# A two-block network on one core: the odd block's projection and its gated linear attention in one phase

## The chip, the cores and the metric

The kernel runs on one core of a Trainium2 chip. TensorE (PE) multiplies matrices, VectorE (DVE), ScalarE (ACT) and GpSimd (POOL) work on elements, SyncE (SP) issues transfers. Each engine takes its instructions in order and waits on semaphores. The metric is the device time of the whole program in microseconds. Before the change the median of three runs is 1949.43 us (1949.24 to 1950.46).

## The reference

Two networks in a row on 256 tokens of width 1024, all in f32: a block of attention and a block of state-space scan with their context, and then a second network of two layers. The change lies in the odd layer of the second one, of which the mixer is this (4 heads, keys of 128, values of 256, chunks of 64, gate rank 16):

```python
def gla_mixer(h, w_in, w_a2, b_a, head_g, w_out):
    z = h @ w_in
    q, k, v, r, ga = jnp.split(z, [hk, 2 * hk, 2 * hk + hv, 2 * hk + 2 * hv], axis=-1)
    log_a = jax.nn.log_sigmoid((ga @ w_a2 + b_a).astype(jnp.float32)) / C_TAU
    o = gla_chunked(heads(q, C_DK) * (C_DK ** -0.5), heads(k, C_DK), heads(v, C_DV), heads(log_a, C_DK))
    o = rms_norm(o, head_g)
    o = o.transpose(0, 2, 1, 3).reshape(Bn, S, hv) * jax.nn.silu(r.astype(jnp.float32))
    return o.astype(h.dtype) @ w_out

# gla_chunked, per chunk of 64 tokens; b = cumsum(log_a) in the chunk
    q_t, k_t, k_s = q * jnp.exp(b), k * jnp.exp(-b), k * jnp.exp(b_last - b)
    attn = jnp.where(causal, q_t @ k_t.T, 0.0)
    o = attn @ v + q_t @ state          # state of the chunks before
    state = exp(b_last) * state + k_s.T @ v
```

Here h is the RMS norm of x. The layer then adds the result to x and runs a convolutional feed-forward network (FFN) over it.

## The kernel before

The program is a chain of phases. Each phase has its own tiles and semaphores, and the next begins when all engines are through. Around the change they are: ffn0 (the FFN of the even layer), odin (the odd layer's input projection, `project`), gla (the attention, `gla`), odout (the output projection, `project_residual`) and ffn1 (`conv_ffn`).

**Products.** Large products run through `Split`. An f32 weight tile of 1024 x 512 lies in one of the two slots of a ring. For each half of it (four of the eight k tiles) ScalarE writes a rounded copy w_lead (L274, `lead`), and VectorE the remainder w_rest (L280, `rest`). x is parted the same way. TensorE then runs three matmuls for one exact product, lead by lead, lead by rest and rest by lead (L363). A group is one weight tile and gives 512 output columns; a half group is 24 matmuls (4 k tiles, 2 token tiles, 3 passes). odin has six groups: q, k, two of v, two of r. There is one buffer for each half of w_lead and w_rest, so the w_lead of a half can be written only when TensorE is through with the same half of the group before. SP loads the next tile into a ring slot as soon as both its w_rest are made. `empty` (L2161) takes a group out of PSUM into zz, with Identity for q, k, v and Silu for r.

**Start of a projection.** TensorE transposes x (L415), ScalarE makes x_lead (L424) and VectorE x_rest (L431). The first half of the first weights has been parted in the phase before: `EarlyHalf`, w_lead on ScalarE (L393) and w_rest on POOL (L397).

**The gates' inputs.** h @ w_ga has 16 columns. It stands behind the last group in odin as f32 matmuls (L2140), then ScalarE copies it to gaT.

**gla.** Its six small tables are loaded at the start of the phase. Then, each step waiting for the one before: gates (PE L2496), log-sigmoid (DVE L2551 to L2559, ACT Exp L2618 and Ln L2620), sums in the chunk (PE L2500, L2501), decays (PE L2504), exponentials (ACT L2623, L2624), q and k scaled (DVE L2563 to L2572), transposes (PE L2511, ACT L2635). Then four heads one after the other: scores (PE L2520), clamp and mask (DVE L2581, L2582), three k.T v products (PE L2527) and states (DVE L2587, L2589), outputs (PE L2535 to L2538), and a copy of the head's output to o (DVE L2594). Then the head norm and the gate r over all heads (DVE L2600 to L2609, ACT Sqrt L2637). At last o is transposed (PE L1931) and parted into mix_lead (ACT L2640) and mix_rest (DVE L1939), which are odout's x. In the middle ScalarE makes the early w_lead for odout, POOL its w_rest.

## Time and profile before

| | |
|---|---|
| median of 3 runs | 1949.43 us |
| profiled execution | 1948.9 us |
| its span | 1947.1 us, mean granted TensorE clock 0.899 |
| PE busy | 1649.0 us (85% of the span) |
| DVE busy | 1028.6 us (53%) |
| ACT busy | 781.0 us (40%) |
| POOL busy | 648.0 us (33%) |
| DMA | 327.98 MB, mean 168 GB/s |

The span runs from the first instruction to the last; the profiled execution's own time is 1.8 us longer. The granted clock is a share of TensorE's 2.4 GHz: 1.0 is that, 0.5 is 1.2 GHz. Busy times are sums over the whole program. The phases around the change lie at about 1566 to 1645 us (odin), 1645 to 1721 (gla), 1721 to 1747 (odout) and 1747 to 1947 (ffn1).

### The profile page before, as it was taken

Reading aid. Unit: us, or ns where it says so; the run is one execution under the profiler, and the core shown is the slowest. Engines: PE = TensorE matmul, PEld = TensorE weight load, DVE = VectorE, ACT = ScalarE, POOL = GpSimd, SP = SyncE. Lnnn points to the kernel's source line nnn. Section 1 sums busy time; section 2 is a strip of 40 time slices with the busy share of each in tenths; the row PEclk is TensorE's granted clock in tenths of the full one; section 3 lists DMA queues with packets and bytes.
Section 4 is the critical chain, followed back from the end, with each engine's and each line's share of the span. In section 5 each row is a group of like instructions: output and inputs, shape, how many; then the busy total and the mean of one; then the engine's idle time right before and its main releaser. Section 6 shows DMA issues by size and latency. Waiting matters only on the chain. (4 is left out here: it accounts for less than half of the span.)

```text
span 1947.1 us, 28034 instructions
## 1 busy us (share of the span) xinstructions
PE 1649.0 (85%) x11254; PEld 1360.9 (70%) x11254; DVE 1028.6 (53%) x1308; ACT 781.0 (40%) x1034; POOL 648.0 (33%) x492
## 2 busy tenths in 40 slices
PE   7858999899698699887568987747999998669998
PEld 1226888778586588776558976636899976359997
DVE  5224442178745246776726545354666642556665
ACT  1212122255513366664353434222554443335442
POOL 0007888499745823998402002000000000000000
PEclk9878999999898888987879998856999999879999
DMA  7754666455524457765856543401544433034441
GB/s 316 274 219 138 244 223 226 169 186 192 198 94 165 121 183 211 212 185 161 207 125 233 186 160 135 153 12 44 199 193 192 173 131 141 1 114 190 194 194 43
DMA packets 132232, 327.98 MB, mean 168 GB/s; under 512 B 31876, under 2 KB 87300, under 8 KB 115988
## 3 DMA queue, kind: packets, MB, share of 16 engines
q1 hardware_dynamic: 126614, 297.66, 44.6%
q10 hardware_dynamic: 5508, 28.77, 4.1%
q8 instruction: 78, 1.28, 0.3%
q14 instruction: 32, 0.26, 0.0%
HBM read 289.85 MB, written 36.55 MB: 168 GB/s over the span
## 5 line engine op out<-in xcount | busy, mean ns | idle before, releaser
L397 POOL TENSOR_TENSOR w_rest<-resident_ring,w_lead 128x2048 fp32r<-128x2048 f32 x7 | 32.3, 4614 | 582.6 <-ACT w_lead L393 393.6
L2732 PE MATMUL ffn_ps<-ffn_x_lead,w_lead 128*128 128x256 f32 x672 | 188.4, 280 | 1.1 <-DVE w_rest L2811 1.1
L2732 PE MATMUL ffn_ps<-ffn_x_lead,w_rest 128*128 128x256 f32 x672 | 188.6, 281 | 0.0
L2732 PE MATMUL ffn_ps<-ffn_x_rest,w_lead 128*128 128x256 f32 x672 | 188.3, 280 | 0.0
L2811 DVE TENSOR_TENSOR w_rest<-resident_ring,w_lead 128x2048 fp32r<-128x2048 f32 x42 | 96.1, 2292 | 83.3 <-ACT w_lead L2776 83.3
L363 PE MATMUL qkvz_ps<-qkvz_w_lead,h_lead 128*128 128x512 f32 x320 | 126.1, 394 | 9.9 <-DVE qkvz_w_rest L280 6.8
L280 DVE TENSOR_TENSOR w_rest<-resident_ring,w_lead 128x2048 fp32r<-128x2048 f32 x33 | 75.7, 2295 | 99.2 <-ACT w_lead L274 99.2
L2732 PEld LDWEIGHTS ffn_ps<-ffn_x_lead,w_lead 128*128 128x128 f32 x672 | 126.1, 188 | 2.2 <-issue 1.5
L2732 PEld LDWEIGHTS ffn_ps<-ffn_x_rest,w_lead 128*128 128x128 f32 x672 | 126.4, 188 | 0.7
L2732 PEld LDWEIGHTS ffn_ps<-ffn_x_lead,w_rest 128*128 128x128 f32 x672 | 126.3, 188 | 0.0
L363 PE MATMUL qkvz_ps<-qkvz_w_lead,h_rest 128*128 128x512 f32 x320 | 125.6, 392 | 0.0
L363 PE MATMUL qkvz_ps<-qkvz_w_rest,h_lead 128*128 128x512 f32 x320 | 125.5, 392 | 0.0
L1874 DVE TENSOR_TENSOR w_rest<-resident_ring,w_lead 128x1024 fp32r<-128x1024 f32 x32 | 49.9, 1566 | 138.5 <-ACT w_lead L1769 138.4
L280 DVE TENSOR_TENSOR qkvz_w_rest<-resident_ring,qkvz_w_lead 128x2048 fp32r<-128x2048 f32 x20 | 51.7, 2591 | 127.8 <-ACT qkvz_w_lead L274 127.8
L1657 PE MATMUL ssm_ps_u<-h_lead,w_lead 128*128 128x512 f32 (+1 forms) x256 | 94.5, 369 | 20.1 <-issue 15.1
L274 ACT ACTIVATE qkvz_w_lead<-resident_ring 128x2048 fp32r<-128x2048 f32 x20 | 38.3, 1924 | 167.0 <-PE qkvz_ps L363 145.6
L529 PE MATMUL ada_ps<-resident_ring,ada_sT 128*2 128x512 f32 x192 | 90.3, 630 | 15.9 <-ACT ada_sT L495 9.0
L274 ACT ACTIVATE w_lead<-resident_ring 128x2048 fp32r<-128x2048 f32 x33 | 63.1, 1915 | 95.2 <-PE odin_ps L363 26.9
L2776 ACT ACTIVATE w_lead<-resident_ring 128x2048 fp32r<-128x2048 f32 x42 | 80.1, 1912 | 50.3 <-PE ffn_ps L2732 50.2
L1641 POOL TENSOR_TENSOR ssm_V<-ssm_ptab,ssm_cc 128x512 f32<-128x512 f32 x52 | 71.3, 1372 | 78.0 <-PE ssm_ps_y L1705 74.3
L1343 POOL TENSOR_TENSOR resident_x<-xc,resident_x 128x512 f32<-128x512 f32 x64 | 93.5, 1461 | 5.0
L1657 PE MATMUL ssm_ps_u<-h_rest,w_lead 128*128 128x512 f32 (+1 forms) x256 | 89.9, 351 | 0.0
(492 smaller groups left out, 4646.7 us busy)
## 6 DMA issues: line engine op xcount, KB each, us to landing
resident_ring<-in_ffn_gu SPq DMA_DIRECT2D x22, 2048.0 KB, 9.0
resident_ring<-in_ada_w SPq DMA_DIRECT2D x12, 2048.0 KB, 7.7
ffn_wd<-in_ffn_down SPq DMA_DIRECT2D x22, 1024.0 KB, 4.9
xc<-s_q_scratch SPq DMA_DIRECT2D x128, 128.0 KB
resident_x<-in_s_bT SPq DMA_DIRECT2D x64, 256.0 KB
resident_ring<-in_attn_w_in ACTq DMA_DIRECT2D x8, 2048.0 KB, 10.7
s_W_scratch<-resident_x SPq DMA_DIRECT2D x64, 256.0 KB, 4.4
resident_ring<-in_s_w SPq DMA_DIRECT2D x32, 512.0 KB, 5.8
```

Of the source, the lines that this page charges most:

```text
L274: self.core.nc.scalar.activation(self.w[0][j], self.core.tile(r)[:, j * HK:(j + 1) * HK, :], ACT.Copy).then_inc(self.lead_made, 1)
L280: self.core.nc.vector.tensor_tensor(self.w[1][j], self.core.tile(r)[:, j * HK:(j + 1) * HK, :], self.w[0][j].bitcast(F32), ALU.subtract).t ...
L363: last = nc.tensor.matmul(bank(parity, t), self.lhs[x][:, half * HK + k, t * P:(t + 1) * P], self.w[w][j][:, k, :], start=(half, k, x, w) ...
L397: self.core.nc.gpsimd.tensor_tensor(self.slots[1][0], self._raw(r), self.slots[0][0].bitcast(F32), ALU.subtract).then_inc(self.rest_made, 1)
L529: last = nc.tensor.matmul(ps[g % 2][0:2], sT[:, k, :], core.tile(g % 2)[:, k, :], start=k == 0, stop=k == KT - 1)
L1343: g.tensor_tensor(b, q(0), b, ALU.mult).then_inc(self.scaled, 1)
L1641: g.tensor_tensor(v, power(c), coef(0), ALU.mult)
L1657: last = nc.tensor.matmul(out, w[:, s, k, :], hparts[x][:, k, cols], start=k == 0 and x == 0 and w is w_lead, stop=k == KT - 1 and w is w_ ...
L1874: v.tensor_tensor(w_rest[:, u % 2], raw, w_lead[:, u % 2].bitcast(F32), ALU.subtract).then_inc(rest_made, 1)
L2732: last = nc.tensor.matmul(ps[s][f][:, m, :], w_part[w][m][:, k, f * P:(f + 1) * P], x_part[x][:, k, :], start=(k, w, x) == (0, 0, 0), stop ...
L2776: nc.scalar.activation(w_part[0][m], raw(s, m), ACT.Copy).then_inc(w_lead_made, 1)
L2811: v.tensor_tensor(w_part[1][m], raw(s, m), w_part[0][m].bitcast(F32), ALU.subtract).then_inc(w_rest_made, 1)
```

## The change

`project` for the odd layer and `gla` become one function and one phase, `odd_mixer`. Its instructions are written out group by group, without loops. `products` gets a hook, `after(g, half)`, that is called when TensorE's half group is issued, and the attention's matmuls are issued from it:

- after (0,0) the gates' inputs, now in three passes of parted operands (xw is parted too, ahead of everything else on ACT and DVE); after (0,1) the gates; after (1,1) the sums; after (2,1) the transposes of q and k
- after (3,0) the decays, scores and states of head 0; after (3,1), (4,0) and (4,1) the outputs of one head and the scores and states of the next; after (5,0) the outputs of head 3.

ScalarE and VectorE do their parts of the attention between their `lead`, `rest` and `empty`. The head norm is done per head: squares with their sum on ScalarE, the factor head_g on POOL (L2512 after), 1/rms and r in one VectorE instruction per head and token tile (`gated`, SCALAR_TENSOR_TENSOR, 128x256, eight in all). POOL's early rest for odout stands behind its fourth gain. All scores, kv and outputs share four PSUM banks; there is one bank for scores in place of two. The six table loads stand ahead of the ring loads on SP. The odd phase now begins and ends with the other ring slot (slot 1), so odout and ffn1 take `flip=1`.

```diff
@@ Split.products @@
-    def products(self, pe, bank, free, part_wait=None, between=None, unrolled=False, soon=None):
+    def products(self, pe, bank, free, part_wait=None, between=None, unrolled=False, soon=None, after=None):
...
                 if between is not None and (g, half) == (0, 0):
                     between()
+                if after is not None:
+                    after(g, half)
@@ odd_mixer @@
+            @block.sync
+            def _(sp):
+                sp.dma_start(xw[:], d["od_w_ga"]).then_inc(xl, 16)
...
+                    sp.dma_start(dst, src).then_inc(loads, 16)
+                split.loads(sp, d["od_w_in"])
+                split.following(sp, d["od_w_out"], first=1)
+
+            @block.gpsimd
+            def _(pool):
+                pool.wait_ge(loads, 96)
+                for h in range(CHD):
+                    pool.wait_ge(o_squared, LT * (h + 1))
+                    nc.gpsimd.tensor_tensor(o[:, :, head(h)], o[:, :, head(h)], g_row[:].unsqueeze(1).to_broadcast([P, LT, CDV]), ALU.mult).then_inc(o_gained, 1)
+                early.rest(pool, 1)
...
+                def scores_and_states(h):
+                    a = h % 2
+                    if h == 0:
+                        pe.wait_ge(ks_done, 1)
+                    if h:
+                        pe.wait_ge(att_done, h)
+                    pe.wait_ge(freed, emptied(2 + h // 2, LT - 1))
...
+                        if h * 3 + c >= 2:
+                            pe.wait_ge(st_done, h * 3 + c - 1)
...
+            @block.scalar
...
+                act.wait_ge(xl, 16)
+                sc.activation(xw_parts[0][:], xw[:], ACT.Copy).then_inc(xw_lead, 1)
+                split.start_scalar(act, norm)
...
+                lead(1, 0)
+                act.wait_ge(ga_mm, 1)
+                sc.activation(gaT[:], ps_x, ACT.Copy).then_inc(ga_done, 1)
+                lead(1, 1)
+                act.wait_ge(rs_made, 1)
+                empty(0, ACT.Identity)
+                for t in range(LT):
+                    act.wait_ge(xs, t + 1)
+                    sc.activation(ex[:, t, :], ex[:, t, :], ACT.Exp, scale=-1.0).then_inc(ex0, 1)
+                for t in range(LT):
+                    act.wait_ge(ex0, t + 1)
+                    sc.activation(ex[:, t, :], ex[:, t, :], ACT.Ln, bias=1.0).then_inc(ex1, 1)
+                lead(2, 0)
...
+                squares(2)
+                split.early_lead(act, early, 1)
+                squares(3)
+                act.wait_ge(o_squared, LT * CHD)
+                sc.activation(rs[:], ms[:], ACT.Sqrt, scale=1.0 / CDV, bias=core.eps[:, 1:2]).then_inc(o_std, 1)
+                empty(5, ACT.Silu)
...
+                def gated(h):
+                    dve.wait_ge(o_gained, h + 1)
+                    for t in range(LT):
+                        last = v.scalar_tensor_tensor(out=o[:, t, head(h)], in0=o[:, t, head(h)], scalar=rs[:, t, h:h + 1],
+                                                      in1=zz[:, t, R0 + h * CDV:R0 + (h + 1) * CDV], op0=ALU.mult, op1=ALU.mult)
+                    last.then_inc(out_done, 1)
@@ conv_ffn, project_residual: ring slot s becomes s ^ flip @@
-                    core.load(sp, s, weights[u + 2])
+                    core.load(sp, s ^ flip, weights[u + 2])
@@ build @@
-                project(core, "odin", "od_w_in", (2 * CK + 2 * CV) // NW, zz, [(ACT.Identity, 4), (ACT.Silu, 2)], "od_w_out", 1, slots,
-                        extra=(d["od_w_ga"], gaT))
-                gla(core, zz, gaT, mix, slots)
-            project_residual(core, "odout", "od_w_out", mix, "ffn_gu0", slots, diag)
...
+            odd_mixer(core, mix, slots)
+            project_residual(core, "odout", "od_w_out", mix, "ffn_gu1", slots, diag, flip=1)
```

The order of the instructions shows the same at three places. In the rows, "x8" is a run of eight alike, and a name before the arrow is what is written. First TensorE at the heads. Before, behind the last projection product and the gates, the first two heads stand together:

```order
L2520 MATMUL gla_ps_a<-gla_qT,gla_kT 128x128 x2
L2527 MATMUL gla_ps_l<-zz,gla_ks 128x256 x3
L2535 MATMUL gla_ps_b<-zz,gla_att 128x256
L2538 MATMUL gla_ps_b<-gla_st,gla_qT 64x256
L2535 MATMUL gla_ps_b<-zz,gla_att 128x256
L2537 MATMUL gla_ps_b<-gla_st,gla_qT 64x256
L2538 MATMUL gla_ps_b<-gla_st,gla_qT 64x256
L2520 MATMUL gla_ps_a<-gla_qT,gla_kT 128x128 x2
L2527 MATMUL gla_ps_l<-zz,gla_ks 128x256 x3
L2535 MATMUL gla_ps_b<-zz,gla_att 128x256
L2538 MATMUL gla_ps_b<-gla_st,gla_qT 64x256
L2535 MATMUL gla_ps_b<-zz,gla_att 128x256
```

After, the outputs of head 0 and the scores and kv products of head 1 (names with odd_) stand behind half group (3,1), with the first products of (4,0) behind them:

```order
L363 MATMUL odd_ps<-w_rest,odd_x_lead 128x512
L363 MATMUL odd_ps<-w_lead,odd_x_rest 128x512
L2580 MATMUL odd_ps_b<-odd_zz,odd_att 128x256
L2583 MATMUL odd_ps_b<-odd_st,odd_qT 64x256
L2580 MATMUL odd_ps_b<-odd_zz,odd_att 128x256
L2582 MATMUL odd_ps_b<-odd_st,odd_qT 64x256
L2583 MATMUL odd_ps_b<-odd_st,odd_qT 64x256
L2561 MATMUL odd_ps_b<-odd_qT,odd_kT 128x128 x2
L2567 MATMUL odd_ps_l<-odd_zz,odd_ks 128x256 x3
L363 MATMUL odd_ps<-w_lead,odd_x_lead 128x512
L363 MATMUL odd_ps<-w_rest,odd_x_lead 128x512
```

So each such piece has 24 matmuls of products ahead of it and 24 behind it. Second, VectorE from its last operation on ks on; before, the heads follow each other directly:

```order
L2572 TENSOR_TENSOR gla_ks<-zz,gla_ks 128x512 x2
L2581 TENSOR_SCALAR gla_att<-gla_ps_a 128x256
L2582 TENSOR_TENSOR gla_att<-gla_att,gla_sums 128x256
L2587 COPY gla_st<-gla_ps_l 128x256
L2589 SCALAR_TENSOR_TENSOR gla_st<-gla_st,gla_dec,gla_ps_l 128x256 x2
L2594 COPY gla_o<-gla_ps_b 128x256 x2
L2581 TENSOR_SCALAR gla_att<-gla_ps_a 128x256
L2582 TENSOR_TENSOR gla_att<-gla_att,gla_sums 128x256
L2587 COPY gla_st<-gla_ps_l 128x256
L2589 SCALAR_TENSOR_TENSOR gla_st<-gla_st,gla_dec,gla_ps_l 128x256 x2
```

After, a w_rest stands ahead of the copy that keeps each head's output:

```order
L2766 TENSOR_TENSOR odd_ks<-odd_zz,odd_ks 128x512 x2
L280 TENSOR_TENSOR w_rest<-resident_ring,w_lead 128x2048
L2708 TENSOR_SCALAR odd_att<-odd_ps_b 128x256
L2709 TENSOR_TENSOR odd_att<-odd_att,odd_sums 128x256
L2714 COPY odd_st<-odd_ps_l 128x256
L2716 SCALAR_TENSOR_TENSOR odd_st<-odd_st,odd_dec,odd_ps_l 128x256 x2
L280 TENSOR_TENSOR w_rest<-resident_ring,w_lead 128x2048
L2723 COPY odd_o<-odd_ps_b 128x256 x2
L2708 TENSOR_SCALAR odd_att<-odd_ps_b 128x256
L2709 TENSOR_TENSOR odd_att<-odd_att,odd_sums 128x256
```

The copy to odd_o and the states of the next head stand in line behind the w_rest of half group (4,0), and so on for three more. Third, VectorE's end of the phase; before:

```order
L2600 TENSOR_TENSOR zz<-gla_o 128x1024
L2601 TENSOR_REDUCE gla_ms<-zz 128x4
L2600 TENSOR_TENSOR zz<-gla_o 128x1024
L2601 TENSOR_REDUCE gla_ms<-zz 128x4
L2604 RECIPROCAL gla_rs<-gla_rs 128x8
L2607 TENSOR_TENSOR gla_o<-gla_o,gla_rs 128x1024
L2608 TENSOR_TENSOR gla_o<-gla_o,gla_g_row 128x1024
L2609 TENSOR_TENSOR gla_o<-gla_o,zz 128x1024
L2607 TENSOR_TENSOR gla_o<-gla_o,gla_rs 128x1024
L2608 TENSOR_TENSOR gla_o<-gla_o,gla_g_row 128x1024
L2609 TENSOR_TENSOR gla_o<-gla_o,zz 128x1024
L1939 TENSOR_TENSOR mix_rest<-gla_ps_l,mix_lead 128x256 x8
```

After:

```order
L2723 COPY odd_o<-odd_ps_b 128x256 x2
L2783 RECIPROCAL odd_rs<-odd_rs 128x8
L2729 SCALAR_TENSOR_TENSOR odd_o<-odd_o,odd_rs,odd_zz 128x256 x8
L2789 TENSOR_TENSOR mix_rest<-odd_ps_l,mix_lead 128x256 x2
L2789 TENSOR_TENSOR mix_rest<-odd_ps_b,mix_lead 128x256 x2
L2789 TENSOR_TENSOR mix_rest<-odd_ps_l,mix_lead 128x256 x2
L2789 TENSOR_TENSOR mix_rest<-odd_ps_b,mix_lead 128x256 x2
```

The squares and their sums have left VectorE, and three multiplications over all heads have become one per head and token tile. What left stands on ScalarE, whose table loads are listed too, with the early half and the exit of the last group around it:

```order
L2633 ACT_TABLE_LOAD
L2633 ACTIVATE odd_zz<-odd_ps,resident_rs 128x512 x2
L2638 ACTIVATE odd_junk,odd_ms<-odd_o 128x256 x2
L395 ACTIVATE w_lead<-resident_ring 128x2048
L2638 ACTIVATE odd_junk,odd_ms<-odd_o 128x256 x2
L2689 ACT_TABLE_LOAD
L2689 ACTIVATE odd_rs<-odd_ms,resident_eps 128x8
L2633 ACT_TABLE_LOAD
L2633 ACTIVATE odd_zz<-odd_ps,resident_rs 128x512 x2
L2693 ACTIVATE mix_lead<-odd_ps_l 128x256 x2
```

Silu, Sqrt and Silu each need their own table there, and the early w_lead for odout (L395) stands ahead of the squares of head 3. Before, one Sqrt table was loaded behind the copies of kT.

## Rows read from the trace of the kernel before

**Rows 1.** Windows: us, busy us of PE, PEld, DVE, ACT, POOL; clock, DMA share, GB/s
```profile
1565.00:1641.00 76.00, 73.42 (x321) 58.27 (x322) 28.97 (x21) 36.20 (x38) 0.00 (x0) 0.98 0.42 160
1641.00:1721.00 80.00, 43.31 (x156) 21.68 (x154) 43.86 (x71) 21.44 (x32) 4.84 (x1) 0.74 0.04 14
1681.00:1701.00 20.00, 14.79 (x64) 6.91 (x60) 9.48 (x24) 0.00 (x0) 0.00 (x0) 0.94 0.00 1
```

**Rows 2.** Timeline, TensorE; start us, us, engine line op, [idle before <-releaser]
```profile
1568.26 0.77 PE L363 MATMUL odin_ps<-w_lead,odin_x_lead 128*128 128x512 f32 x1 [0.20 <-DVE odin_x_rest L431]
1568.83 0.63 PE L363 MATMUL odin_ps<-w_rest,odin_x_lead 128*128 128x512 f32 x1
1569.26 0.63 PE L363 MATMUL odin_ps<-w_lead,odin_x_rest 128*128 128x512 f32 x1
...
1637.05 0.39 PE L363 MATMUL odin_ps<-w_lead,odin_x_rest 128*128 128x512 f32 x1
1637.36 0.61 PE L2140 MATMUL odin_ps_x<-odin_x_lead,odin_xw 128*16 128x256 f32 x2
...
1721.35 0.79 PE L363 MATMUL odout_ps<-w_lead,mix_lead 128*128 128x512 f32 x1 [1.26 <-DVEq L302]
```

**Rows 3.** Timeline: TensorE at the second group; VectorE at one w_rest
```profile
1582.20 0.47 PE L363 MATMUL odin_ps<-w_lead,odin_x_lead 128*128 128x512 f32 x1 [0.70 <-DVE w_rest L280]
...
1600.99 2.29 DVE L280 TENSOR_TENSOR w_rest<-resident_ring,w_lead 128x2048 fp32r<-128x2048 f32 x1 [3.22 <-ACT w_lead L274]
```

**Rows 4.** Start of the projection: SP, ScalarE; transfer (KB each, us to landing)
```profile
1566.63 0.33 SPq L2107 DMA_DIRECT2D odin_xw<-in_od_w_ga  x1
...
1567.12 0.84 ACT L424 ACTIVATE odin_x_lead<-odin_ps,resident_norm_g 128x256 fp32r<-128x256 f32 x2 [7.33 <-PE odin_ps L415]
...
odin_xw<-in_od_w_ga SPq DMA_DIRECT2D x1, 64.0 KB, 1.7
```

**Rows 5.** Timeline, TensorE: transposes in the products; last sums, decays
```profile
1572.25 0.60 PE L415 MATMUL odin_ps<-resident_ident,resident_x 128*128 128x128 f32 x4
...
1573.04 0.47 PE L363 MATMUL odin_ps<-w_lead,odin_x_lead 128*128 128x512 f32 x1
...
1663.53 1.02 PE L2501 MATMUL gla_ps_l<-gla_la,gla_block_ones 128*128 128x512 f32 x2
1664.38 1.84 PE L2504 MATMUL gla_ps_d<-gla_ends,gla_la 128*128 128x2 f32 x16
```

**Rows 6.** Timeline, TensorE, third head: scores, first outputs, next head's scores
```profile
1688.07 0.71 PE L2520 MATMUL gla_ps_a<-gla_qT,gla_kT 128*128 128x128 f32 x4
...
1691.57 0.67 PE L2535 MATMUL gla_ps_b<-zz,gla_att 128*128 128x256 f32 x2 [0.69 <-issue]
...
1693.96 0.71 PE L2520 MATMUL gla_ps_a<-gla_qT,gla_kT 128*128 128x128 f32 x4
```

**Rows 7.** Timeline, ScalarE and VectorE: gate chain
```profile
1645.12 1.28 ACT L2618 ACT_TABLE_LOAD   x1 [0.27 <-PEq L2100]
1654.16 0.63 ACT L2618 ACTIVATE gla_ex<-gla_ex 128x512 f32<-128x512 f32 x1 [7.76 <-DVEq L2554]
...
1652.13 0.75 DVE L2551 SCALAR_TENSOR_TENSOR gla_la<-gla_ps_b,resident_rs,gla_ba 128x512 f32<-128x512 f32 x1 [21.36 <-PE gla_ps_b L2496]
...
1654.22 0.75 DVE L2551 SCALAR_TENSOR_TENSOR gla_la<-gla_ps_b,resident_rs,gla_ba 128x512 f32<-128x512 f32 x1
```

**Rows 8.** POOL and VectorE side by side; one line (min/median/max ns)
```profile
1667.55 4.84 POOL L397 TENSOR_TENSOR w_rest<-resident_ring,w_lead 128x2048 fp32r<-128x2048 f32 x1 [103.05 <-ACT w_lead L393]
...
1668.63 0.69 DVE L2568 TENSOR_TENSOR gla_ks<-gla_ps_l,gla_ks 128x512 f32<-128x512 f32 x1
...
L2572 DVE TENSOR_TENSOR gla_ks<-zz,gla_ks x2: 692/1773/2854, 1670.1 to 1673.0; 128x512 f32<-128x512 f32 x2
```

**Rows 9.** Lines of VectorE, 1565 to 1722 us; busy us, mean ns, idle before
```profile
L2589 DVE SCALAR_TENSOR_TENSOR gla_st<-gla_st,gla_dec,gla_ps_l 128x256 f32<-128x256 f32 x8 | 3.8, 480 | 1.5 <-PE gla_ps_l L2527 1.4
...
L1939 DVE TENSOR_TENSOR mix_rest<-gla_ps_l,mix_lead 128x256 fp32r<-128x256 f32 x8 | 3.4, 424 | 3.6 <-ACT mix_lead L2640 3.6
```

More of the change, by code:

```diff
@@ L2183, in _ @@
             def _(sp):
-                split.following(sp, d[following])
+                split.following(sp, d[following], first=flip)
             @block.gpsimd
             def _(pool):
-                early.rest(pool, 0)
+                early.rest(pool, flip)
             @block.scalar
@@ new lines, in decays @@
+                def decays():
+                    pe.wait_ge(qkT_done, 4)
+                    for t in range(LT):
+                        for h in range(CHD):
+                            last = nc.tensor.matmul(ps_d[:, h, t, :], la[:, t, h * CDK:(h + 1) * CDK], ends[:], start=True, stop=True)
+                    last.then_inc(dec_mm, 1)
+                def scores_and_states(h):
+                    a = h % 2
+                    if h == 0:
[3 more added lines that the diff above has]
+                    pe.wait_ge(freed, emptied(2 + h // 2, LT - 1))
@@ new lines, in _ @@
+                norm.transposes(pe, 0)
+                split.products(pe, lambda s, t: ps[s][t][:], [(freed, LT)], lambda k: pe.wait_ge(norm.rest_made, k + 1), unrolled=True,
+                               soon=lambda: norm.transposes(pe, 1), after=after)
+                pe.wait_ge(o_done, CHD)
+                for f in range(KT):
+                    if f % 2 == 0:
+                        pe.wait_ge(out_done, f // 2 + 1)
+                    if f >= 4:
+                        pe.wait_ge(mix_rest, f - 3)
+                    for t in range(LT):
+                        last = nc.tensor.transpose(banks[f % 4][:, t * P:(t + 1) * P], o[:, t, f * P:(f + 1) * P], core.ident[:])
+                    last.then_inc(o_turned, 1)
@@ new lines, in _ @@
+                dve.sem_inc(qk_done, 1)
+                rest(3, 0)
+                for t in range(LT):
+                    dve.wait_ge(qk_exp, t + 1)
+                    last = v.tensor_tensor(ks[:, t, :], zz[:, t, K0:V0], ks[:, t, :], ALU.mult)
+                last.then_inc(ks_done, 1)
+                rest(3, 1)
+                dve.wait_ge(dec_done, 1)
+                states(0)
+                rest(4, 0)
+                keep(0)
+                states(1)
+                rest(4, 1)
+                keep(1)
@@ L2638, in _ @@
+                states(2)
+                rest(5, 0)
+                keep(2)
+                states(3)
+                rest(5, 1)
+                keep(3)
+                dve.wait_ge(o_std, 1)
+                chain.run(v.reciprocal(rs[:], rs[:]))
+                for h in range(CHD):
+                    dve.wait_ge(freed, emptied(4 + h // 2, LT - 1))
+                    gated(h)
                 for f in range(KT):
-                    act.wait_ge(S["o_turned"], f + 1)
-                    sc.activation(mix[0][:, f, :], ps_l[f % 2][:, 0:NL], ACT.Copy).then_inc(S["mix_lead"], 1)
@@ L2700, in _ @@
                 def _(pool):
[L2701 removed]
+                    early.rest(pool, 1 - flip)
             @block.tensor
```

335 lines of the change are left out of this document (192 added, 143 removed).

## The prediction

> **What bounds the kernel now.** I read the windows by stage first [rows 1]. The projection of the odd block keeps TensorE busy for 73.42 of 76 us at a granted clock of 0.98. In the 80 us behind it, the gated linear attention, it is busy for 43.31 us at 0.74, VectorE for 43.86, ScalarE for 21.44, and next to nothing is transferred. No engine bounds that stage: a chain from engine to engine does. The marks on TensorE's own timeline give the sizes [rows 2]: first product at 1568.26, the last product's successor at 1637.36, first product of the output projection at 1721.35. So 69.1 us for twelve half groups of weights, then 84.0 us in which only attention moves. Inside the projection VectorE and ScalarE are more than half idle: VectorE makes a w_rest in 2.29 us and waits 3.22 us before the next, 5.5 us a turn [rows 3]. The change puts the 84 us into those gaps.
>
> **The sum, up to TensorE's last product.** Start mark: 1568.26. All times below are on the clock of the profile before.
>
> Start, +1.5 us. ScalarE now has to wait for the transfer of xw before its first instruction. SP issues it at 1566.63, it lands 1.7 us later, and the copy of 128x128 costs some 0.3: 1568.6, against 1567.12 for the first x_lead before [rows 4]. VectorE and TensorE shift by the same.
>
> Products, 68.4 us. 69.1 less the wait of 0.70 ahead of the second group [rows 3], which the gate matmuls now fill. One half group is 24 matmuls at 0.229, the 5.5 us of rows 3.
>
> Inserted on TensorE, 11.6 us. Gate inputs: 24 matmuls of the kind of the products, with 256 columns for 512, so half of 0.229 us each, 2.8 us; before, 16 f32 matmuls stood there. Gates and sums: six f32 matmuls of 512 columns, 0.85 us from the row of the last pair to its successor [rows 5], 0.9 with the start, 5.4. Sixteen transposes: 0.79 us for eight, 1.6 [rows 5]. Decays: 1.84 [rows 5].
>
> Heads, 21.5 us. Before, a head takes 5.9 us [rows 6]: scores 0.64, states, wait for VectorE, last state 0.6, wait, outputs 2.4. Now the second wait falls behind a half group of products, but the first stays: the third kv matmul waits for the first state copy, and VectorE must first keep the head before (0.2 after the outputs, 0.7), clamp, mask and copy (0.45, 0.35, 0.45). That is 2.1 us after the outputs, then 0.6 to 0.9 for the last kv matmul. So 2.4 + 3.0 = 5.4 us per piece for three pieces, 2.9 for head 0, where only the decays' exponential (0.19) comes ahead, and 2.4 for the last outputs. The order shows these pieces at the five places. 16.2 + 2.9 + 2.4 = 21.5.
>
> Cuts, +0.7. The stream is cut at nine places. The one such switch in the trace costs 0.31 instead of 0.23 us from start to start (the row at 1637.05 and its successor, rows 2), 0.08 each. Bounds: 0, and 0.7 us each, the idle "issue" time ahead of L2535 in the heads [rows 6], 6.3 in all. I take the switch, as it is the same kind of cut.
>
> Last product at 1568.3 + 1.5 + 68.4 + 11.6 + 21.5 + 0.7 = 1672.0, last outputs at 1666.5.
>
> **Is the work of the others ready?** The tight place is the gates. TensorE ends half group (0,1) at 1585.6; ScalarE copies w_lead (0.35 + 1.9), VectorE makes w_rest (2.3): 1590. Then la, ex and max twice (2.1 us from one la to the next [rows 7]), Exp, a table load of 1.28, two Ln, and 1.6 for the first la: 1598.3. TensorE wants it at 1598.4. The next pair, 1599.9 against 1600.2, and w_rest of (2,0), 1602.2 against 1602.0. There is no reserve: each us of delay there is a us of time. The table load ahead of an Exp does not wait with it: before, it ran at 1645.12 and its Exp at 1654.16 [rows 7]; if it did, 1.3 us more. From the second group of heads on VectorE has some 5 us of idle time ahead of each kept head, so the w_rest that stand ahead of it in its queue are hidden. POOL's three early gains are off the path. The moved ring loads have whole groups of time; SP's six small loads now stand ahead of them in its queue, some 3 us of issue, and the first ring load is due only when the w_rest of half group (0,1) is made.
>
> **The tail.** From the last outputs: keep 0.9 (1667.4), two squares with sum 0.9 (1668.3). Then two branches. ScalarE: table load and Sqrt 1.6, reciprocal 0.2, ready at 1670.2. POOL: gain of head 3, 512 columns, a quarter of the 2048 of the early rest's 4.84 us [rows 8] and a start, 1.3, so 1669.7; right behind it early.rest, 4.8 us, to 1674.5. That collides with gated: its operands are o and zz, both in SBUF. In the trace, L2572, with two SBUF inputs, took 0.69 us once and 2.85 us the other time, when it began at 1670.08 under POOL's 1667.55 to 1672.39 [rows 8]: it came to its end only after POOL. A VectorE operation with one input in PSUM (L2568, 1668.63) that began under the same POOL instruction took the usual 0.69 [rows 8]. L2572 is TENSOR_TENSOR; gated is SCALAR_TENSOR_TENSOR, which no row shows in this position. Bounds: 0 (as if it read PSUM) and 4.3 us (blocked until POOL ends). I take 4.3, the row with the same operands. Then eight gated at 0.45 (0.42 to 0.48 [rows 9]), 3.6, eight mix_rest at 0.42 [rows 9], 3.4, and 0.4 into the next phase: 1674.5 + 7.4 = 1681.9. Transposes and mix_lead run beside them.
>
> On this the Trainium skill, "SBUF — State Buffer", section "Who interferes with whom", speaks against the change: a VectorE instruction with two SBUF inputs and a GpSimd instruction that reads SBUF exclude each other, the second waits for the whole of the first. It names no exception for the scalar form. By it the sum is 1910; the opposite is the first rival.
>
> 1721.35 - 1681.9 = 39.4 us saved. Everything behind it (output projection, FFN) keeps its instructions, only the ring slots swap. A Sqrt table must now be loaded in the output projection, since Silu came last: 1.28 us [rows 7], while ScalarE waits for the last half of x; I count nothing, a few tenths at most. Profiled execution: 1948.9 - 39.4 = 1909.5. The median of the runs is 0.5 above the profiled execution, so I predict 1910.
>
> **Rivals.**
> A, the port does not bind. gated starts at 1670.2, the tail ends 4.3 us earlier: 1906. For: the Sqrt branch and POOL's start stand half a us apart, and VectorE may be first. Against: the row of L2572. 0.20.
> B, the cuts and the gate chain cost more. Each cut at 0.7 in place of 0.08, 5.6 us, and one table load behind its wait, 1.3: 1917. For: no reserve in the gate chain. Against: the one switch in the trace. 0.15.
> C, slower than before, by TensorE's clock. Half groups cut by waits of about 1 us might let the granted clock fall to 1.2 GHz. At that level matmuls stand 0.43 us apart [rows 2], a half group costs 10.3 instead of 5.5; from eight of the twelve on, the 39.4 us are nearly all gone; with eleven and the inserted work doubled in part it is 52 + 20 - 39, about 1980. Against: in 1681 to 1701, in the midst of the heads, TensorE had 14.79 us of work in 20 and was granted 0.94 [rows 1]; now it has more. 0.03.
>
> The Trainium skill, "TensorE: Matmul & The Clock Gate", Part 1, has the clock follow how busy the array has been of late. By that too C is unlikely, as TensorE is denser now than in 1681 to 1701.
>
> **Numbers.** Forecast 0.61, A 0.20, B 0.15, C 0.03, something else 0.01. The range: A less 2 us for inserted matmuls that I took too dear, 1903.5; B plus 1, 1918. Left out are C, the upper third of B, and the ends of A, about 0.15. This kernel's runs differ by 1.2 us, so no change means within 0.2%, 4 us. Faster 0.95, same 0.02, slower 0.03.
>
> **What would show it.** First product at about 1569.8; granted clock near 1.0 up to 1672; between half groups from (3,0) on pieces of 5.4 us with one wait of about 1 us for the first state copy; sums following (1,1) with a wait under 1 us; in the tail TensorE idle for about 4 us, VectorE's first gated several us long and ending with POOL's early rest. A wait on TensorE for la or w_rest of more than 2 us, or a clock below 0.9, would make it wrong.

## The result and the profile after

| | before | after |
|---|---|---|
| median, runs | 1949.34 us, 4 (1944.8 to 1950.46) | 1899.73 us, 4 (1893.75 to 1901.42) |
| ratio | | 0.9744, 95% interval 0.9718 to 0.977 |
| profiled execution, its span | 1948.9, 1947.1 us | 1899.7, 1897.9 us |

The kernel became faster, as forecast, but 10.3 us below the 1910.0 and 3.8 us below the range. The odd layer itself went almost to plan. Its first transposes and the first product of the output projection bound a stretch that holds all that the change touches. First TensorE's timeline of before (start, duration, engine, line, operation, and the idle time ahead with what ended it); the other end is the last of [rows 2], 1721.35:

```profile
1566.68 0.63 PE L415 MATMUL odin_ps<-resident_ident,resident_x 128*128 128x128 f32 x4 [2.13 <-PEq L109]
```

The same engine after, with the places that the prediction spoke of:

```profile
1558.04 0.68 PE L417 MATMUL odd_ps<-resident_ident,resident_x 128*128 128x128 f32 x4 [2.13 <-PEq L109]
1561.15 0.76 PE L363 MATMUL odd_ps<-w_lead,odd_x_lead 128*128 128x512 f32 x1 [1.58 <-DVE odd_x_rest L433]
...
1590.84 1.02 PE L2534 MATMUL odd_ps_b<-odd_la,odd_sums 128*128 128x512 f32 x2
...
1594.07 0.59 PE L363 MATMUL odd_ps<-w_lead,odd_x_lead 128*128 128x512 f32 x1
...
1624.10 0.60 PE L2580 MATMUL odd_ps_b<-odd_zz,odd_att 128*128 128x256 f32 x2
...
1626.42 0.71 PE L2561 MATMUL odd_ps_b<-odd_qT,odd_kT 128*128 128x128 f32 x4
1627.06 0.70 PE L2567 MATMUL odd_ps_l<-odd_zz,odd_ks 64*128 64x256 f32 x4
1628.47 0.70 PE L2567 MATMUL odd_ps_l<-odd_zz,odd_ks 64*128 64x256 f32 x2 [0.71 <-DVE odd_st L2714]
1629.10 0.50 PE L363 MATMUL odd_ps<-w_lead,odd_x_lead 128*128 128x512 f32 x1
...
1658.20 0.50 PE L363 MATMUL odd_ps<-w_lead,odd_x_lead 128*128 128x512 f32 x1
...
1666.75 0.63 PE L2619 MATMUL odd_ps_l<-resident_ident,odd_o 128*128 128x128 f32 x4 [2.81 <-DVE odd_o L2729]
...
1672.66 0.79 PE L363 MATMUL odout_ps<-w_lead,mix_lead 128*128 128x512 f32 x1 [1.26 <-DVEq L302]
```

From mark to mark the stage was 154.67 us long (1721.35 less 1566.68) and is 114.62 (1672.66 less 1558.04): 40.05 us shorter, where the prediction had 39.4. Behind it, from the output projection's first product to the end of the span, 225.8 us became 225.2. That is 40.6 of the 49.2 us between the two spans. The other 8.6 lie ahead of the stage, in instructions that the change doesn't touch: the same transposes begin at 1558.04 and not at 1566.68.

The windows of the stage (us; busy us of PE, PEld, DVE, ACT, POOL; granted clock, DMA share, GB/s) answer to [rows 1]:

```profile
1558.00:1664.00 106.00, 101.45 (x452) 74.55 (x452) 57.30 (x75) 55.58 (x78) 7.75 (x5) 0.95 0.34 125
1664.00:1673.00 9.00, 3.81 (x17) 2.83 (x18) 8.01 (x16) 3.98 (x10) 1.93 (x1) 0.71 0.00 0
1616.00:1620.00 4.00, 3.70 (x9) 2.50 (x10) 3.24 (x4) 0.39 (x1) 0.00 (x0) 0.57 0.10 41
```

TensorE, busy for 43.31 of the attention's 80 us before, is now busy for 101.45 of 106. The granted clock is 0.95 over that stretch. It stands near the level of 1.2 GHz in the first 7 us (0.54 over 1558 to 1565), is 1.00 from there to 1616, falls once, for some 4 us behind the first head (the third window), and is 1.00 again up to 1667; in the tail it falls once more (0.50 over 1668 to 1673). And the waits of TensorE in the stage (who for whom, total us, times, longest), which are all that there are over 1 us:

```profile
PE odd_ps_l L2567 <- DVE odd_st L2714: 2.9, 4, 0.8
PE odd_ps_l L2619 <- DVE odd_o L2729: 2.8, 1, 2.8
PE odd_ps L417 <- PEq L109: 2.1, 1, 2.1
PE odd_ps L363 <- DVE odd_x_rest L433: 1.6, 1, 1.6
PE odout_ps L363 <- DVEq L302: 1.3, 1, 1.3
PE odd_ps_l L2619 <- DVE mix_rest L2789: 1.1, 1, 1.1
```

No wait for la, w_rest or a ring load is among them. The third line is the seam between phases, as before. (PEq and DVEq are the instruction sequencers of TensorE and VectorE; "issue", further down, marks a wait for which the profile shows no releaser.)

The tail shows the collision that the sum had counted. The timeline of POOL and VectorE:

```profile
1660.10 1.30 POOL L2512 TENSOR_TENSOR odd_o<-odd_o,odd_g_row 128x512 f32<-128x512 f32 x1 [7.90 <-ACT odd_junk L2638]
1661.34 4.59 POOL L399 TENSOR_TENSOR w_rest<-resident_ring,w_lead 128x2048 fp32r<-128x2048 f32 x1
...
1661.91 7.07 DVE L2729 SCALAR_TENSOR_TENSOR odd_o<-odd_o,odd_rs,odd_zz 128x256 f32<-128x256 f32 x8
```

and the line of the gated operations (min/median/max ns):

```profile
L2729 DVE SCALAR_TENSOR_TENSOR odd_o<-odd_o,odd_rs,odd_zz x8: 471/472/4303, 1661.9 to 1668.5; 128x256 f32<-128x256 f32 x8
```

The first gated operation begins at 1661.91 and takes 4.30 us, to the end of POOL's early rest at 1665.93 and some 0.3 more; the other seven take 0.47. It is the picture of L2572 in [rows 8]. The Trainium skill, "SBUF — State Buffer", section "Who interferes with whom", has a VectorE instruction with two SBUF inputs and a GpSimd instruction that reads SBUF block each other; this trace agrees for the scalar form too, with 4.30 against 0.47 us.

### The profile page after: what moved, and what is told of

Its sections match the earlier page's. It is cut to its first block and busy times, and to the rows that moved or that the text cites. A ratio compares the mean times of both kernels' runs of the same rounds, so it can differ in the third digit from the quotient of the medians.

```text
span 1897.9 us, 28023 instructions
## 1 busy us (share of the span) xinstructions
PE 1632.5 (86%) x11246; PEld 1354.3 (71%) x11246; DVE 1020.8 (54%) x1307; ACT 783.4 (41%) x1051; POOL 647.1 (34%) x496
## 3 DMA queue, kind: packets, MB, share of 16 engines
q8 instruction: 78, 1.28, 0.3%
```

## Experiments

All ratios are to before on the same chip. "Stage" is the stretch between the two marks above, "front" what lies ahead of it. A kernel with one run has one profiled execution; its stage is read, not its total.

### Where do the 8.6 us ahead of the stage come from?

Three answers: they differ from execution to execution of any kernel; they hang on how the program is laid out or how long it is; they hang on when TensorE begins. Four kernels on one chip, ten timed runs of each of the first three and four of the last.

**b_same** is before, unchanged. **b_tail** is before with 48 small instructions more, behind all work:

```diff
+            @block.vector
+            def _(dve):
+                for n in range(48):
+                    nc.vector.memset(pad[:, n:n + 1], 0.0)
```

**b_shift** and **a_shift** are before and after with TensorE's first matmul held back until another transfer has landed, 14.5 to 14.7 us into the span instead of 8.9 (twice the hold of some 3 us that the expectations name):

```diff
                 pe.wait_ge(s_silu, 1)
+                pe.wait_ge(ident_in, 16)
                 for g in range(TAB):
```

> The kernel before once more, unchanged. Open is why the changed kernel ran its unchanged first 1558 us in 8.6 us less. Theory T1 (TensorE's granted clock in the unchanged part falls and rises at places that differ from execution to execution): the profile shows the end of ffn0 somewhere between 1550 and 1566 us, not where it stood. T2 (tied to the program): ffn0 ends within 1 us of where it ended in the first profile, the clock falls again at 27.9 and rises at 34.3 us, and the time is 1949 to 1950.

> The kernel before with 48 tiny memsets on VectorE in the last phase, beside the store of the output. Nothing ahead of the store changes. T2a (what stands late in the program, its length or placement, moves the early part): the first 1560 us change by several us either way. T1 or T2b (only what runs early matters): as the kernel before within 1 us, apart from run to run spread.

> The kernel before with TensorE's first matmul held until the identity matrix has landed, some 3 us later (12 in place of 9 us). The early phase is bound by transfers for the most part, so less than 3 us of it should stay. T3 (the clock's falls and rises depend on where the work stands in time, so that any shift early in the program redraws them): the clock steps at 28 to 34 and 520 to 533 us move by more than the shift, and the sum of the first 1560 us changes by -8 to +8 us, not by the +1 to +3 of the shift alone. Rival (a plain delay): +1 to +3 us and all later clock steps shifted by just that.

> The changed kernel with the same early hold of some 3 us. T3: the first 1558 us change by -2 to +10 us, towards the values of the kernel before; the odd phase itself keeps its 114.6 us from the first transpose to the first output product within 0.5. Rival (the 8.6 us belong to the change): the first part stays 8 us shorter than in the kernel before with the same shift.

| | median (range) us | ratio, interval | front | stage | behind |
|---|---|---|---|---|---|
| b_same | 1941.16 (1932.78 to 1950.8) | 0.9996 (0.9966 to 1.0026) | 1560.2 | 154.6 | 225.8 |
| b_tail | 1940.53 (1933.92 to 1946.34) | 1.0006 (0.9984 to 1.0028) | 1555.4 | 154.9 | 225.7 |
| b_shift | 1939.83 (1935.03 to 1945.75) | 1.0002 (0.998 to 1.0024) | 1557.6 | 154.8 | 225.8 |
| a_shift | 1895.37 (1892.69 to 1902.52) | 0.9758 (0.972 to 0.9795) | 1560.7 | 114.7 | 225.3 |

Before itself, in 25 runs beside these, has a median of 1939.82 and goes from 1932.54 to 1950.12. So the same program spreads over 18 us, and the 1949.43 of three runs that the prediction started from lies near the upper end. In the profiled executions nearly all of it is in the front: stage and tail repeat within 0.3 us, and the same transposes begin at 1566.68, 1560.16, 1555.44 and 1557.62. Two of these rows, of b_same and of b_tail:

```profile
1560.16 0.63 PE L415 MATMUL odin_ps<-resident_ident,resident_x 128*128 128x128 f32 x4 [2.13 <-PEq L109]
```

```profile
1555.44 0.63 PE L415 MATMUL odin_ps<-resident_ident,resident_x 128*128 128x128 f32 x4 [2.13 <-PEq L109]
```

With the same hold, the front of the changed kernel was 3.0 us longer than that of before (1560.65 against 1557.62) and not 8 us shorter, so the 8.6 us as a whole don't belong to the change. Neither 48 instructions more at the end of the program nor a later beginning of TensorE changes anything that these runs can tell (a_shift against the after of the first table: stage 114.7 for 114.6); program layouts that differ more were not tried.

What differs inside the front is in part how long TensorE takes for the same matmuls. The windows from 20 us to the first transposes of before and then of b_same, and a window of 25 us inside them, one program in two executions (columns as above):

```profile
20.00:1566.68 1546.68, 1306.52 (x9312) 1080.52 (x9310) 814.17 (x1045) 614.57 (x858) 638.39 (x486) 0.89 0.52 176
515.00:540.00 25.00, 13.25 (x50) 10.47 (x50) 19.06 (x10) 11.51 (x7) 17.20 (x8) 0.73 0.66 242
```

```profile
20.00:1560.16 1540.16, 1299.62 (x9312) 1073.42 (x9310) 814.08 (x1045) 614.72 (x858) 638.29 (x486) 0.90 0.52 176
515.00:540.00 25.00, 14.39 (x62) 11.67 (x61) 19.74 (x11) 11.89 (x8) 16.54 (x6) 0.80 0.66 242
```

For the same 9312 matmuls TensorE was busy 6.9 us less in b_same, while VectorE and ScalarE repeat within 0.2, and the front is 6.5 us shorter. In the short window before was granted 0.73 and issued 50 matmuls, b_same 0.80 and 62. But the busy time alone doesn't order the fronts: a_xw, below, has 1297.82 us of it and a front of 1561.3. What decides which execution gets which clock, and how much of the 11 us between the four fronts it makes up, no run here tells.

### Which waits are left in the stage?

Each of four kernels changes one thing in after. **a_pool** holds POOL's early rest back until the last gated operation:

```diff
+                pool.wait_ge(out_done, CHD)
                 early.rest(pool, 1)
```

> The changed kernel, POOL's early rest held until the eighth gated is done. Read by the stage, first transpose of the odd phase to first product of the output projection, 114.6 us in the changed kernel. Theory (gated was blocked by POOL's read of SBUF): the first gated falls from 4.30 to 0.47 us; POOL now runs 4.6 us behind gated and ends the phase, 0.4 + 4.6 + 0.4 us after the last gated, so the stage is 2.0 us shorter, 112.6, not 3.8. Rival (the 4.3 us are something else, as a first instruction's own cost): first gated stays long, and the stage grows by 2 to 5 us as POOL's work moves back.

Stage 113.4, so 1.2 us won of the 2.0 expected. The lock is gone, the gated operations take 1.67 us for four, but two waits take its place. TensorE's rows, then VectorE's and POOL's, of a_pool:

```profile
1670.43 0.68 PE L2620 MATMUL odd_ps_l<-resident_ident,odd_o 128*128 128x128 f32 x4 [2.04 <-DVE mix_rest L2790]
...
1674.94 0.79 PE L363 MATMUL odout_ps<-w_lead,mix_lead 128*128 128x512 f32 x1 [3.14 <-DVEq L302]
```

```profile
1665.48 1.67 DVE L2730 SCALAR_TENSOR_TENSOR odd_o<-odd_o,odd_rs,odd_zz 128x256 f32<-128x256 f32 x4
1668.27 1.67 DVE L2730 SCALAR_TENSOR_TENSOR odd_o<-odd_o,odd_rs,odd_zz 128x256 f32<-128x256 f32 x4 [1.12 <-ACT odd_zz L2634]
...
1670.02 4.51 POOL L399 TENSOR_TENSOR w_rest<-resident_ring,w_lead 128x2048 fp32r<-128x2048 f32 x1 [5.06 <-DVE odd_o L2730]
```

The gate r of the last group is now late by 1.12, and the rest itself ends at 1674.53, so the output projection waits 3.14 instead of 1.26. The lock had made the first gated operation 3.8 us longer; taking it away was worth 1.2 as long as this work stood on POOL.

**a_state** moves the first two state steps ahead of clamp and mask on VectorE:

```diff
-                    chain.run(v.tensor_scalar(att[:, a], ps_a, 3.0e38, -3.0e38, ALU.min, ALU.max))
-                    v.tensor_tensor(att[:, a], att[:, a], sums[:].unsqueeze(1).to_broadcast([P, LT, P]), ALU.mult).then_inc(att_done, 1)
                     for c in range(3):
+                        if c == 2:
+                            chain.run(v.tensor_scalar(att[:, a], ps_a, 3.0e38, -3.0e38, ALU.min, ALU.max))
+                            v.tensor_tensor(att[:, a], att[:, a], sums[:].unsqueeze(1).to_broadcast([P, LT, P]), ALU.mult).then_inc(att_done, 1)
```

> The changed kernel with VectorE's first two state steps ahead of clamp and mask in each head. Theory (TensorE's remaining wait in each head is for the first state copy behind keep, clamp and mask): the wait of 0.71 us in four pieces goes to under 0.2, the stage is 2.0 to 2.8 us shorter, 112.2. Rival (the wait is the turnaround of PSUM and semaphores): it stays at 0.5 or more, or comes back at the outputs as a wait for the mask, and the stage stays within 0.5 us.

Stage 114.3: 0.3 us of the 2.4 expected, a miss. TensorE's wait fell only from 0.71 to 0.58, as its row in a_state shows:

```profile
1622.69 0.70 PE L2567 MATMUL odd_ps_l<-odd_zz,odd_ks 64*128 64x256 f32 x4
1623.97 0.70 PE L2567 MATMUL odd_ps_l<-odd_zz,odd_ks 64*128 64x256 f32 x2 [0.58 <-DVE odd_st L2715]
```

The copy needs the first kv product, and that stands behind the scores. Moved forward it waited 0.57 us for TensorE: the chain is kv, copy, kv, and VectorE's other work was hardly in it.

**a_xw** parts xw behind x on ScalarE and VectorE:

```diff
+                split.start_scalar(act, norm)
                 act.wait_ge(xl, 16)
                 sc.activation(xw_parts[0][:], xw[:], ACT.Copy).then_inc(xw_lead, 1)
-                split.start_scalar(act, norm)
...
+                split.start_vector(dve, norm)
                 dve.wait_ge(xw_lead, 1)
                 v.tensor_tensor(xw_parts[1][:], xw[:], xw_parts[0][:].bitcast(F32), ALU.subtract).then_inc(xw_rest, 1)
-                split.start_vector(dve, norm)
```

> The changed kernel with the parting of xw behind that of x on ScalarE and VectorE. Theory (ScalarE's wait for xw's transfer is 1.4 us at the start of the phase): first product 1.6 us after the first transpose as in the kernel before, in place of 3.1, the stage 1.3 us shorter, 113.3. Rival (the first half group is bound by something else, or the gates' inputs now come late): first product earlier but the time is lost ahead of the gates' inputs, stage within 0.5 us.

Stage 113.7, 0.9 of the 1.3 expected, and the wait of the first product fell from 1.58 to 0.32:

```profile
1562.90 0.76 PE L363 MATMUL odd_ps<-w_lead,odd_x_lead 128*128 128x512 f32 x1 [0.32 <-DVE odd_x_rest L433]
```

The start itself won more than that, 2.3 us: the first product comes 1.59 us behind the first transposes for 3.11, and the twelve products from it to the second transposes take 4.02 us for 4.77, as fewer of them run at the lower clock. But 1.3 of it went again behind head 0, where the lower clock lasted longer in this execution. The same window of a_xw and then of after:

```profile
1616.00:1624.00 8.00, 7.25 (x21) 5.04 (x21) 4.44 (x6) 1.47 (x1) 0.00 (x0) 0.57 0.18 76
```

```profile
1616.00:1624.00 8.00, 7.70 (x26) 5.79 (x27) 3.50 (x4) 0.39 (x1) 0.00 (x0) 0.79 0.06 23
```

Head 0 and the half group behind it take 12.84 us in a_xw and 11.58 in after. Whether the change or chance made that stretch longer, one execution can't tell.

**a_lump** takes the spreading back in part: heads 1 to 3 stand in one piece behind half group (3,1), so the same work is inserted, but not between half groups.

```diff
-                        scores_and_states(1)
-                    if (g, half) == (4, 0):
-                        outputs(1)
...
+                        for h in range(1, CHD):
+                            scores_and_states(h)
+                            outputs(h)
...
-                rest(4, 1)
...
+                keep(3)
+                rest(4, 1)
+                rest(5, 0)
                 rest(5, 1)
-                keep(3)
```

> The changed kernel with the heads 1 to 3 in one piece behind half group (3,1), not one between each two half groups; VectorE's w_rest of (4,1), (5,0), (5,1) behind them. Theory (a head waits twice for VectorE, 0.7 and 0.7 us, and the half group between its states and its outputs hides only the second wait): three times about 0.7 to 0.8 more, and TensorE waits for the w_rest of (4,1), little; stage about 117. The last head is kept long before the end, so squares and gains leave the tail: up to 3 us back, as the early lead and rest then come first. Rival (the interleaving of the heads is what saves the most of the 40 us): stage 124 or more.

Stage 121.2, 6.6 us longer: more than the 117 of the sum, less than the rival's 124. Outputs now wait again for their own head's last state, 0.69 us three times; TensorE's row at the second of them in a_lump:

```profile
1639.84 1.13 PE L2580 MATMUL odd_ps_b<-odd_zz,odd_att 128*128 128x256 f32 x2 [0.69 <-issue]
```

and two windows of it, each around the outputs of a head:

```profile
1632.00:1638.00 6.00, 5.25 (x18) 2.27 (x18) 1.83 (x6) 0.00 (x0) 0.28 (x1) 0.72 0.00 0
1639.00:1645.00 6.00, 5.31 (x19) 2.34 (x18) 1.52 (x4) 0.00 (x0) 0.00 (x0) 0.72 0.00 0
```

Besides the fall around head 0, which is there as in after, the granted clock falls twice in the lump, to 0.72 over 6 us; in after the pieces at 1634 to 1656 ran at 1.00. That is the part that the sum did not have. The outputs of heads 1 and 2, in these stretches, take 3.85 and 3.93 us up to the next scores; those of head 3, at 1.00, take 2.39 up to the next product. So the two falls cost 3.0 us. The waits of 0.69 (2.1), the falls (3.0) and a tail that is 1.2 longer make 6.3 of the 6.6. The tail was expected to be up to 3 us shorter. But ScalarE's order was left as it was: the squares of head 3, kept at 1650.6, ran only at 1668.36, behind the early w_lead, and the last gain and the lock came behind them as in after.

### A version without these waits

**a_kv** draws the lesson of a_state: the first two kv matmuls go ahead of the scores on TensorE too. VectorE's part is that of a_state, and its wait for the scores moves with clamp and mask.

```diff
-                    for t in range(LT):
-                        last = nc.tensor.matmul(ps_a[:, t, :], kT[:, h, t * P:(t + 1) * P], qT[:, h, t * P:(t + 1) * P], start=True, stop=True)
-                    last.then_inc(att_mm, 1)
                     for c in range(3):
+                        if c == 2:
+                            for t in range(LT):
+                                last = nc.tensor.matmul(ps_a[:, t, :], kT[:, h, t * P:(t + 1) * P], qT[:, h, t * P:(t + 1) * P], start=True, stop=True)
+                            last.then_inc(att_mm, 1)
...
```

**a_rest** draws that of a_pool: the early rest moves to VectorE, into its idle 2.6 us ahead of the reciprocal.

```diff
-                early.rest(pool, 1)
...
                 keep(3)
+                dve.wait_ge(early.lead_made, 1)
+                v.tensor_tensor(slots[1][0], core.tile(1)[:, 0:HK, :], slots[0][0].bitcast(F32), ALU.subtract).then_inc(early.rest_made, 1)
```

**a_best** is both, and a_xw. **a_same** is after, unchanged, beside it.

> The changed kernel with the two first kv matmuls of each head ahead of its scores, and the first two state steps ahead of clamp and mask on VectorE. The run that only moved the state steps cut TensorE's wait from 0.71 to 0.58 us, since the first kv matmul then came too late. Theory (the wait is the chain kv, copy, kv, and the scores can cover it): the wait for the first state copy goes to under 0.15 us in all four heads and the stage is 2.9 us shorter, 111.7. Rival (VectorE's keep of the head before sets the copy's start): the wait stays at 0.4 or more, stage 113 or longer.

> The changed kernel with the early rest half on VectorE, 2.3 us between the last kept head and the reciprocal, where it has been idle for 2.6 us, and none on POOL. The run that held POOL's early rest back until the last gated operation freed the 4.3 us but made the output projection wait 3.1 us for that rest itself. Theory: first gated under 0.5 us or held only until the last gain on POOL ends, output projection's wait about 1.3 us again, stage 111.6 (1.8 below the held POOL). Rival (Silu of the last group sets the tail): the stage is 113 or longer, with VectorE waiting for zz for 2 us or more.

> The changed kernel with three waits of its odd phase taken away together: the parting of xw goes behind that of x on ScalarE and VectorE (the one part of this already seen alone: first product's wait 1.6 to 0.3 us, stage 1.0 shorter); in each head's piece the two first kv matmuls stand ahead of the scores and VectorE makes its first two states ahead of clamp and mask; and the early rest half leaves POOL for VectorE, between the last kept head and the reciprocal. Theory: the three lie at different places of one chain and add up, 1.0 + 2.9 + 3.0, so the odd phase, from its first transpose to odout's first product, is 107 to 109 us long for 114.6, and the median of the runs stands some 7 us below that of the changed kernel on this chip, about 0.972 of before. Rival: what is won in the pieces is lost again at a w_rest or at the gate chain, which had no reserve; the stage would be 111 us or more, with a new wait of TensorE for w_rest or la.

> The changed kernel, word for word. For its own spread and its ratio to before on one chip beside the version with the three waits taken away. Theory (the unchanged part before the odd phase ends at another place in each execution, the saving is 40 us): median 1897 to 1903 where before shows 1937 to 1943, ratio 0.977 to 0.981, and single runs over at least 8 us. Rival (the change also speeds what stands ahead of it): ratio 0.974 or lower and single runs within 3 us.

| | median (range) us | ratio, interval | stage |
|---|---|---|---|
| a_same | 1898.75 (1893.53 to 1902.61), 6 | 0.9777 (0.9743 to 0.9811) | 114.6 |
| a_kv | 1897.56, 1 | | 110.1 |
| a_rest | 1898.06, 1 | | 111.6 |
| a_best | 1889.96 (1879.33 to 1896.83), 6 | 0.9727 (0.9688 to 0.9766) | 106.2 |

a_kv: the wait is gone in all four heads. TensorE's rows of it at the second head, to set beside 1626.42 to 1629.10 above:

```profile
1626.32 0.70 PE L2568 MATMUL odd_ps_l<-odd_zz,odd_ks 64*128 64x256 f32 x4
1626.95 0.71 PE L2563 MATMUL odd_ps_b<-odd_qT,odd_kT 128*128 128x128 f32 x4
1627.60 0.70 PE L2568 MATMUL odd_ps_l<-odd_zz,odd_ks 64*128 64x256 f32 x2
```

The stage is 4.5 us shorter, 1.6 more than expected. About 1.5 of that lies at the first head: the half group behind it takes 5.63 us for 6.83, and its last kv matmul 0.3 less, as in this execution the granted clock did not fall there. In a_best it did again, so this part cannot be counted on. The other 3.0 are what was expected.

a_rest: 3.0 us shorter, 111.6 as expected. Its VectorE and POOL:

```profile
1660.39 2.28 DVE L2782 TENSOR_TENSOR w_rest<-resident_ring,w_lead 128x2048 fp32r<-128x2048 f32 x1
...
1663.31 1.99 DVE L2728 SCALAR_TENSOR_TENSOR odd_o<-odd_o,odd_rs,odd_zz 128x256 f32<-128x256 f32 x4
...
1661.50 2.33 POOL L2512 TENSOR_TENSOR odd_o<-odd_o,odd_g_row 128x512 f32<-128x512 f32 x1 [7.90 <-ACT odd_junk L2637]
```

Now POOL is the one that waits, 2.33 for 1.30 us, until VectorE's rest ends at 1662.67; that costs the gated operations 0.3 (1.99 for 1.67).

a_best: 8.4 us shorter than after, for the 5.6 to 7.6 expected. The three alone gave 0.9, 4.5 and 3.0, which makes 8.4 too, but that is partly chance: around head 0 the clock had taken 1.3 from a_xw and given 1.5 to a_kv. In a_best that stretch is much as in after (the half group 6.74 us for 6.83), and its rows give 2.2 at the start, 3.1 at the heads and 3.1 in the tail. The part that was expected too small is the start, 1.0. The median of a_best is 8.8 us below that of a_same on the same chip. The intervals of the two ratios overlap a little, so the whole times alone don't settle it; the stage, which doesn't depend on the front, does. It is the fastest version here. TensorE's waits that are left in its stage:

```profile
PE odd_ps L417 <- PEq L109: 2.1, 1, 2.1
PE odd_ps_l L2619 <- DVE mix_rest L2792: 2.0, 1, 2.0
PE odout_ps L363 <- DVEq L302: 1.3, 1, 1.3
PE odd_ps L363 <- DVE odd_x_rest L433: 0.4, 1, 0.4
```

a_same came at 0.9777, within what was expected, and its single runs lie 9 us apart. With eleven runs of before beside it, this is the fairer figure for the change than the 0.9744 of the first table.

## Why the prediction was wrong in the total and right in the stage

**The step that failed** is the base: "Profiled execution: 1948.9 - 39.4 = 1909.5", and with it "This kernel's runs differ by 1.2 us". They differ by 18. Three runs that agreed within 1.2 us stood near the slow end, the executions of after near the middle of theirs. With the median of before over 25 later runs, 1939.8, the same sum gives 1900.4, for 1899.73 measured. Between the two profiled executions, 8.6 us of the miss of 9.8 lie in the front and 1.2 in the stage and behind it. The range was built from the unknown costs of the stage alone; the front, four fifths of the time, was held fixed, and that alone put the result outside. In part this was bad luck: only 4 of the 37 later runs reach 1949.24, so that three in a row would come about once in 800 times if each were drawn for itself (an estimate from the 4 in 37). Whether something held those three together, such as the chip or the hour, is open; on each of the three chips of the experiments before reached that height at least once (1950.12, 1949.99, 1950.94).

Point by point, on the clock of after from the first product on (1561.15):

- Start, +1.5: from first transposes to first product 1.58 before and 3.11 after; 1.53. The copy of xw waited for its transfer, as said.
- Inserted, 11.6: gate inputs 2.7, gates and sums 1.9 and 3.2, transposes 1.7, decays 1.7; 11.2.
- Heads, 21.5: head 0 3.0, pieces 5.0 three times for 5.4 (1624.10 to 1629.10, and twice more), last outputs 2.3; 20.3. The wait is 0.71 (0.75 in head 0), the prediction had about 1.
- Products and cuts, 69.1: 71.1. Of the 2.0 more, 1.2 are the half group behind head 0 at the lower clock (6.83 for 5.6 us) and 0.8 the first twelve products (1561.15 to 1565.92, 4.77 us; 1568.26 to 1572.25 before, 3.99). The sum took these over from before; but behind the longer wait of the start more of them ran at the lower clock, in all eight profiled executions with that wait (4.77 to 5.00) and not in a_xw and a_best (4.02 and 4.06). So the start cost 2.3, not 1.5. Each cut cost 0.1 or less: the other half groups take 5.56 to 5.62 with their start. The bound of 0.7 per cut was far off, since that row of before is no cut: it comes back as 0.69 in a_lump, where outputs again follow their own head's last state, and nowhere in after.
- Last product 102.2 us behind the first, measured 102.6. Too dear and too cheap cancelled in part.
- Gates: the two la were made at 1590.2 and 1591.7, in time for the sums at 1590.84 and 1592.56. No wait at all, a reserve of 0.6 us. The table load ran ahead of its Exp, at 1581.10.
- Tail: from the end of the last outputs to the output projection 14.5 us for 15.4. The lock was sized 4.3 from the start of the first gated operation to POOL's end; it measured 4.0 (1661.91 to 1665.93), and 3.8 by the operation's length (4.30 for 0.47). The others stand 0.40 apart, not 0.45.
- Behind, nothing counted: 0.5 us shorter. The Sqrt table load, 1.28 us at 1696.12, stood ahead of the first Sqrt, and ScalarE still waited 0.39 us for the last part of x behind it.

**Rivals.** A (the port does not bind) fell with L2729; that the total came out below A's 1906 has nothing to do with it. Its price of 4.3 was too high as well: with the lock away and the early rest hidden, a_rest won 3.0. B (cuts and gate chain dearer) fell with the waits listed above. C fell in size: one fall of the clock of some 4 us, not eight half groups. That the 8.6 us belong to the change fell with the four fronts of before and with a_shift against b_shift. How much the change moves the front is not quite settled: over all runs the mean of before is 1941.2 (37 runs) and of after 1898.0 (14, a_shift among them), 43.2 apart, and stage and what lies behind it give 40.6. The first transposes begin at 1560.0 on average in four profiled executions of before's front and at 1558.7 in ten of after's. A difference of 1 to 3 us may be there or not; these runs can't tell it from the spread.

## What to carry to other kernels

Work out a change against its own stage, from a mark ahead of it to one behind, and give the rest of the program a spread of its own: three runs within 1 us don't bound that. Where a wait is to be hidden, find both its ends; one end alone moved the wait and won an eighth (a_state) or three fifths (a_pool) of what was expected, both ends won all of it (a_kv 3.0 of 2.9 without the clock's share, a_rest 3.0 of 3.0). Here pieces of some 5 us that wait for another engine fitted between half groups of 5.6 us at almost no cost beyond their own work, where the same pieces in a row (a_lump, one execution) also lost clock. Before two savings are added up, set each against its own rows: a fall of the clock elsewhere took or gave as much as the savings here.

## What the runs showed of the hardware

- One program, one core: 1931.4 to 1950.9 us over 37 runs of before, single executions all over that range, while in its profiled executions the stage of 155 us and the 226 us behind it repeat within 0.3 us.
- Around head 0 the granted clock fell in nine of the ten profiled executions of changed kernels, 0.57 over 4 us in after and 0.57 over 8 us in a_xw, but not in a_kv, whose order there is that of a_best, where it fell. Between the later pieces, with one wait of 0.71 us each, it stayed at 1.00; in a_lump's row of heads it fell twice more.
- A wait of 1.6 to 1.9 us ahead of the first product, in place of 0.2 to 0.4, also made the first twelve products 0.8 to 1.0 us longer (4.77 to 5.00 for 3.99 to 4.06).
- A VectorE operation with two SBUF inputs and one scalar per partition is held by GpSimd like a plain one (4.30 for 0.47 us), and GpSimd's by VectorE's (2.33 for 1.30). In after it also happened where nobody waited for it: the w_rest at 1650.96 took 3.38 us for 2.29, beside GpSimd's third gain at 1650.90.
